# Squares for the DeltaNet norms as float16 high and low halves, summed by float16 products

## The reference

```
def l2norm(x):
    x32 = x.astype(jnp.float32)
    return x32 * lax.rsqrt(jnp.sum(x32 * x32, axis=-1, keepdims=True) + RMS_EPS)

def gated_deltanet_mixer(qkv, a_in, b_in, conv_w, a_log, dt_bias):
    qkv = jax.nn.silu(causal_depthwise_conv(qkv, conv_w))
    q, k, v = jnp.split(qkv, 3, axis=-1)
    q = l2norm(split_heads(q, B_HEADS, B_HEAD_DIM)) * (B_HEAD_DIM ** -0.5)
    k = l2norm(split_heads(k, B_HEADS, B_HEAD_DIM))
    ...
```

## Time and profile before

| | us |
|---|---|
| median of 3 runs | 652.02 |
| all runs | 651.27, 655.02, 652.02 |
| the profiled execution, its own time | 654.71 |
| its span (first to last instruction) | 652.6 |
| mean granted TensorE clock in it | 0.974 |
| PE busy | 589.1 (90% of the span) |
| DVE / ACT / POOL busy | 394.3 / 333.5 / 222.6 |

### The profile page before, as it was taken

The page is one execution under the profiler, slowest core; times in us unless marked ns, Lnnn a source line. Parts: engine busy times, 40 slices in busy tenths (PEclk is TensorE's granted clock), DMA queues, the critical chain, the costliest instruction groups (busy, mean ns, idle before and its releaser), DMA issues.

```text
span 652.6 us, 10019 instructions
## 1 busy us (share of the span) xinstructions
PE 589.1 (90%) x3763; PEld 368.8 (57%) x3763; DVE 394.3 (60%) x889; ACT 333.5 (51%) x585; POOL 222.6 (34%) x161
## 2 busy tenths in 40 slices
PE   3969988999999996999999999988988799799998
PEld 2424556756548653677677777754554466333443
DVE  6401487451687965786876557447799765577311
ACT  4625654425688768350812525346766677243510
POOL 0133453333044466042531530422221464242520
PEclk9998999989999899799999999979999999999999
DMA  8254764443113232120211110111120211162411
GB/s 321 63 127 111 155 123 130 138 153 113 51 50 113 66 98 65 33 65 2 65 33 32 53 46 1 46 53 51 36 78 34 66 33 43 56 228 74 145 55 48
DMA packets 31168, 53.04 MB, mean 81 GB/s; under 512 B 2743, under 2 KB 13201, under 8 KB 31121
## 3 DMA queue, kind: packets, MB, share of 16 engines
q1 hardware_dynamic: 30961, 52.27, 27.7%
q10 hardware_dynamic: 160, 0.14, 0.1%
HBM read 49.98 MB, written 2.42 MB: 80 GB/s over the span
## 4 chain that ended last, share of the span: by engine, by line
PE 67%; DVE 14%; ACT 8%; issue 5%; POOL 2%; DMA 2%; SPq 2%; DVEq 0%; ACTq 0%; PEldq 0%; POOLq 0%
PE bank L1790 12%; PE bank L1603 10%; PE bank L1605 9%; PE bank L1604 9%; PE bank L1858 5%; PE bank L1860 5%; PE bank L1862 5%; ACT stage L735 3%; PE bank L1639 2%; DMA stage<-in_w_in 2%; PE bank L1682 2%; POOL w_lo L518 1%; PE bank L1988 1%; PE bank L1821 1%; PE bank L1761 1%
## 5 line engine op out<-in xcount | busy, mean ns | idle before, releaser
L518 POOL TENSOR_TENSOR w_lo<-stage,w_hi 128x1024 f16<-128x1024 f32 (+4 forms) x76 | 149.1, 1964 | 250.9 <-ACT w_hi L743 250.9
L1790 PE MATMUL bank<-work 128*128 128x128 f32 x616 | 80.1, 280 | 8.1 <-DVEq L1298 7.8
L1790 PEld LDWEIGHTS bank<-work 128*128 128x128 f32 x616 | 77.7, 195 | 17.1 <-DVEq L1298 9.9
L743 ACT ACTIVATE w_hi<-stage 128x1024 f16<-128x1024 f32 (+4 forms) x76 | 74.5, 981 | 18.8 <-issue 14.4
L735 ACT ACTIVATE stage<-stage,small 128x512 f32<-128x512 f32 (+4 forms) x120 | 73.6, 662 | 8.1 <-DMA stage<-in_w_in 8.0
L1858 PE MATMUL bank<-hT_hi,w_hi 128*128 128x512 f16 x192 | 74.5, 388 | 1.7 <-PE bank L1862 0.9
L1860 PE MATMUL bank<-hT_lo,w_hi 128*128 128x512 f16 x192 | 74.2, 387 | 0.5 <-PE bank L1605 0.2
L1862 PE MATMUL bank<-hT_hi,w_lo 128*128 128x512 f16 x192 | 74.1, 386 | 0.3 <-PE bank L1605 0.2
L1603 PE MATMUL bank<-w_hi,hT_hi 128*128 128x260 f16 (+4 forms) x192 | 62.7, 327 | 9.1 <-POOL w_lo L518 6.4
L1604 PE MATMUL bank<-w_lo,hT_hi 128*128 128x260 f16 (+4 forms) x192 | 62.5, 326 | 0.0
L1605 PE MATMUL bank<-w_hi,hT_lo 128*128 128x260 f16 (+4 forms) x192 | 62.5, 325 | 0.0
(11 more groups left out here) (319 smaller groups left out, 1183.6 us busy)
## 6 DMA issues: line engine op xcount, KB each, us to landing
stage<-in_w_in SPq DMA_DIRECT2D x40, 512.0 KB, 3.5
stage<-in_c_phi_w SPq DMA_DIRECT2D x8, 512.0 KB, 4.0
stage<-in_w_branch SPq DMA_DIRECT2D x8, 512.0 KB, 3.7
stage<-in_w_out SPq DMA_DIRECT2D x8, 512.0 KB, 3.8
stage<-in_w_in SPq DMA_DIRECT2D x8, 260.0 KB, 2.8
strips<-rel_rows SPq DMA_DIRECT2D x8, 256.0 KB, 7.3
late<-in_x SPq DMA_DIRECT2D x1, 2048.0 KB, 10.1
out_x<-late SPq DMA_DIRECT2D x8, 256.0 KB, 2.0
```

The costliest lines, as they stand in the source:

```text
L518: gp.tensor_tensor(piece_view(w_lo[:, k % PAIRS, :], c), piece_view(stage[:, piece_at[c, j] % STAGES, :], c), piece_view(w_hi[:, k % PAIRS ...
L743: nc.scalar.activation(piece_view(w_hi[:, k % PAIRS, :], c), full, ACT.Copy).then_inc(hi_ready, 1)
L1790: ins = mm(ps[:, h * P:(h + 1) * P], lhs(h), rhs(h), start=True, stop=True)
```

## The change

For m = 0 to 7 the float32 square is now represented by two float16 numbers. ScalarE makes the high half, with one more ACTIVATE (`Square`, float16 output) right behind each `silu_conv(m)`; since it reads what that instruction wrote, it waits for it. GpSimd still makes the full square, now into `square_full`, waits for itself and for ScalarE's half, and subtracts the high half to get the low one. TensorE adds up both halves, eight float16 products with `ones_half` per m in the place of four float32 products. Sums 0 to 2 now stand after tile 1 of B3 and sum 3 after tile 3 of B3, in front of the "kcT" transpose; nothing stands between the tiles of B4. GpSimd's `squares_b(3)` moves up, between the second and third quarter of B4. Sums 4 to 7 stay inside tile 1 of B2.

```
         squares = early[:, 0:2048]
+        square_full = [early[:, 512 * n:512 * n + 512] for n in range(2)]
+        square_parts = early[:, 1024:3072].bitcast(f16).rearrange("p (s a n) -> p s a n", s=4, a=2)
...
             def squares_b(m):
                 gp.wait_ge(conv_done, m + 1)
-                if m >= 4:
-                    gp.wait_ge(sums_taken, m - 3)
-                gp.tensor_tensor(squares[:, 512 * (m % 4):512 * (m % 4) + 512], qkvT[:, m, 3:T + 3], qkvT[:, m, 3:T + 3],
-                                 ALU.mult).then_inc(SQ.sem, 1)
+                hold(gp.tensor_tensor(square_full[m % 2], qkvT[:, m, 3:T + 3], qkvT[:, m, 3:T + 3], ALU.mult))
+                gp.wait_ge(sq_hi_ready, m + 1)
+                gp.tensor_tensor(square_parts[:, m % 4, 1, :], square_full[m % 2], square_parts[:, m % 4, 0, :],
+                                 ALU.subtract).then_inc(SQ.sem, 1)
...
             for t in range(4):
                 follow(CH_B3, t)
-            squares_b(3)
+                if t == 1:
+                    squares_b(3)
...
                 nc.scalar.activation(qkvT[:, m, 3:T + 3], conv_bank[m % 2][:, :], ACT.Silu).then_inc(conv_done, 1)
+                if m < 8:
+                    act.wait_ge(conv_done, m + 1)
+                    if m >= 4:
+                        act.wait_ge(sums_taken, m - 3)
+                    nc.scalar.activation(square_parts[:, m % 4, 0, :], qkvT[:, m, 3:T + 3], ACT.Square).then_inc(sq_hi_ready, 1)
...
-            project(CH_B3, "B3", True)
+            def square_sums(ms):
+                ps = V.bank("sums")
+                for m in ms:
+                    SQ.wait(pe, ("B", m))
+                    for t in range(NT):
+                        c0 = 32 + 16 * (m // 4) + 4 * t + m % 4
+                        for a in range(2):
+                            ins = mm(ps[:, c0:c0 + 1], square_parts[:, m % 4, a, t * P:(t + 1) * P], ones_half[:, 0:1],
+                                     start=a == 0, stop=a == 1)
+                    ins.then_inc(sums_taken, 1)
+
+            def between_b3(t):
+                if t == 1:
+                    v_bank("sums")
+                    square_sums(range(3))
+                if t == 3:
+                    square_sums([3])
+
+            project(CH_B3, "B3", True, between=between_b3)
```

More of the change, by code:

```diff
@@ L166, in trunk @@
         ones = sb("ones", [P, P])
+        ones_half = sb("ones_half", [P, 2], f16)
         par = sb("par", [P, N_ROWS])
@@ L310, in trunk @@
         z_ready, sums_taken, gsum_ready = sem("z_gates_ready"), sem("squares_summed"), sem("log_decay_ready")
+        sq_hi_ready = sem("squares_hi_ready")
         gtri_ready = sem("cumulative_input_ready")
@@ L510, in hold @@
                 gp.wait_ge(p_step, step[0])
+            gp.memset(ones_half[:, :], 1.0)
             gp.memset(ones[:, :], 1.0).then_inc(fills, 1)
@@ L1812, in key_products @@
                 four(("qk", c), kc_, qc)
[L1815 to L1828, removed]
             def between_b2(t):
@@ L1843, in within_b2 @@
                     square_sums([4 + k // 2])
-            project(CH_B4, "B4", True, between=between_b4)
+            project(CH_B4, "B4", True)
             project(CH_B2, "B2", False, between=between_b2, within=within_b2)
```

## The result

The change makes the kernel slower. The changed kernel takes 659.04 us (median of 4 runs, 658.41 to 659.84), the kernel before 652.38 beside it (4 runs, 651.27 to 655.02): ratio 1.0091, 95% interval 1.0071 to 1.0111. The prediction was 657.4 (652.6 to 660.5), with 0.64 for slower by more than 0.5%. The profiled execution took 658.41, its span is 656.6.

A forecast was written before the change was run, and what follows sets the result against it. The prediction took the chain through ScalarE and GpSimd to L1273 and L1304, not TensorE, as the bound. 1.1 + 2.3 + 2.0 = +5.4 us gave 657.4 from the 652.02 median (660.1 from the profiled execution), range 652.6 to 660.5.

The forecast's parts named there:

- ScalarE: Squares behind silu in B1, B3 and B4: +1.14, +0.57 and +1.14, in all +2.85 us at B4's tile 0; m = 6 +0.7.
- The gap: ScalarE's 3.10 us idle before B4's tile 1 closes as TensorE is early, leaving 2.85 - 3.10 = -0.25 us.
- GpSimd's pairs: Square plus subtraction, 2.15 us per m (2.05 to 2.25); in B2 TensorE waits for them, +1.1 us at L1273.
- TensorE's sums: Eight float16 products take 0.25 us per m; TensorE gains about 4.4 us in B4 and 2.2 in B2.
- Keys' norm: VectorE's small compressed-keys instructions wait for GpSimd, making conv(4) and silu 4 late: +2.3 us (0 to 3).
- Norm factors: VectorE's small instructions behind L1273 wait for GpSimd's work up to its lo_split: +2.0 us (0 to 2.8).
- Rival 4: Clock falls to 1.2 GHz in B2's tile 1 while TensorE waits: +1.8 us, so 659.2; chance 0.12.
- Rival 3: Faster: ScalarE's gap closes, nothing replaces it; 649.4 us, decided at 1.45 us per GpSimd pair in B2; chance 0.08.
- the signs that the prediction named: No 3 us idle before B4's tile 1, about 2 before silu 4, slow VectorE instructions, waits at sums 4 to 7, B4 at full clock.

The follow-up runs named there:

- x5: Changed kernel with squares_b(3) back behind B4's fourth quarter and its sum after B4's tile 0; 657.44 us, ratio 1.0061 to the kernel before.
- x7: Changed kernel with GpSimd's first lo_split of G0 made to wait for the first decay matrix; 656.45 us, ratio 1.0058 to the kernel before.
- x9: Changed kernel with square 3 back behind B4's quarters, its sum after B4's tile 0, and G0's first lo_split behind the norm-factor chain; 656.01 us, ratio 1.0042.
- x6: Kernel before, its places kept, with GpSimd's one square written as float16 and one float16 product on TensorE, no low halves; 650.93 us, ratio 0.9963.
- x4: Changed kernel without low halves: GpSimd neither squares nor subtracts for m = 0 to 7, TensorE makes one product; 651.61 us, ratio 0.9975.

## Why the prediction came out right, step by step

The direction, the place and the mechanism were right. The total hides two errors of opposite sign, a stall taken 1.2 us too long and a gap taken 1.6 us too long, so that it came within 0.5 us (5.4 predicted, 5.9 by the ratio) is in part luck.

- **ScalarE.** Each Square takes 0.63 us as the earlier trace rows said. In B1 the two cost 0.92 on the ruler, not 1.14. At the drain of B4's tile 0 ScalarE is 3.67 us late, of which 1.06 are the keys' stall, so 2.61 for the Squares where 2.85 stood. Up to the last `lo_split` of B2 m = 6 adds 0.65, for 0.7.
- **The gap.** It closed in full, as predicted. But "3.10" was a property of one execution. In the second profile of before it is 1.48. The step that failed is "the gap closes and 2.85 - 3.10 = -0.25 is left": right against the profiled execution, and 1.6 us too favourable against the median. Carrying the sum over to the median by subtracting 2.69 us from the total took no account of where these 2.69 lie, and 1.6 of them lay in the stage of the change.
- **GpSimd's pairs.** Predicted 2.15 (2.05 to 2.25), measured 2.24 (232.15 to 238.87 for three); the four took 9.04 us (232.15 to 241.19), for 8.6. From the drain of B4's tile 1 to the copy of the sums the time grew by 23.82 - 22.16 = 1.66 us; predicted 1.35. The waits of 0.56 to 1.12 at the sums are as described.
- **TensorE's sums.** Eight float16 products take 0.35 us from first to last, for 0.25 predicted, and 24 take 0.75, so 0.03 each. The Trainium skill's 107 ns per load (TensorE: Matmul & The Clock Gate, LDWEIGHTS) would make 24 of them 2.6 us, as an estimate; the row decides, as it did in the prediction. It changes nothing in the sum, since TensorE waits.
- **Keys' norm.** Predicted 2.3, measured 1.06 as ScalarE's wait and 1.24 by taking it away. This is the mis-sized term. L1018 and L1235 were held to the ends of GpSimd's square (205.76) and subtraction (206.99), L1238's first instruction to that of the `lo_split` behind them (208.12); but two others passed in between, L1020 (TENSOR_SCALAR, 31 x 1) even while the subtraction ran. The seven were through at 208.3, where quarter 3's split was just starting, and not at 210.0.
- **Norm factors.** Predicted 2.0, measured 6.95 - 4.78 = 2.17, and 1.96 by taking it away.

Against the profile on which it was built the sum is +5.4 predicted and +4.33 measured: +2.05 and +0.50 at the drain of B4's tile 1, +1.35 and +1.66 up to the copy of the sums, +2.0 and +2.17 in the chain. Against the second profile of before the +5.91 are accounted for by runs to within 0.1: 1.24 keys' norm (x5), 1.88 norm factors (x7; 1.96 against the second profile of the changed kernel), and 2.71 that remain in x9: 0.83 at the drain of B4's tile 1 for the Squares net of the gap, 1.66 for GpSimd's pairs in B2, and 0.22 in the chain, where L1286 still takes 0.42 instead of 0.18. The Squares' share and the pairs' are read from places in the trace; no run took away one of them alone.

Behind the first decay matrix nothing is gained or lost: from there to the end of the span it is 407.0 and 407.3 us in the two profiles of the changed kernel and 407.0 and 406.7 in those of before. Rival 4, the clock falling in B2's tile 1, did not occur: the windows from 220 to 240 are at 1.00, even though TensorE is busy only 6.01 and 6.89 us in them. In x5 and x7 the clock did fall in the window from 220 to 230 (0.83), and neither stage was longer for it: x7 stands at the copy of the sums where the changed kernel does, within 0.1 us. Rival 3's turning point, 1.45 us a pair, was not measured; one float16 square of about 1.0 us per m (x6) and nothing at all (x4) both lie on its faster side, and both kernels are faster than before.

Of the signs that the prediction named, these came: no idle time before B4's tile 1, the wait before silu 4 (1.06 us for about 2), TensorE's waits at sums 4 to 7, and small VectorE instructions of 0.5 to 2 us, though only some of them. One did not: B4 did not run at full clock. The window from 210 to 220 is at 0.87, and with the one before it that makes 3.4 us at 1.2 GHz. It cost nothing here, since ScalarE came to the drain of tile 1 without idle time all the same.

## What to carry to other kernels

Shorter work on an engine pays only up to the next engine in line: here some 4 us less work on TensorE (584.2 us busy; 588.1 in the second profile of before, 589.1 in the first) became waiting, since the engine that had to prepare its operands, GpSimd, was already full for 9.5 of 10 us. A long instruction on GpSimd has a second price, paid by small VectorE instructions beside it: look for chains of 0.2 us instructions on the path and keep GpSimd quiet while they run, with work that isn't due yet behind them and not ahead. And where the profiled execution lies away from the median, find out with a second profile in which stage the difference sits before a gap in that stage is spent.

## What the hardware showed unexpectedly

- The same 32 float32 products, behind the same work to within 0.04 us, took 5.52 and 3.63 us in two executions of the same kernel, with 6.8 and 3.4 us at 1.2 GHz in the window. What decides between the two was not found.
- Small VectorE instructions differ in what they wait for. Beside a GpSimd subtraction a TENSOR_SCALAR of 31 x 1 took 0.14 us and a TENSOR_TENSOR of 31 x 1 behind it 0.84; a COPY of 128 x 16 took 2.11 beside a `lo_split` and 0.17 without.
- Beside VectorE's additions of the indexer's scores GpSimd's square takes 1.49 us instead of 1.04 and its subtraction 1.48 instead of 1.15 (from 193.78 on), while three of those additions take 4.22, so 1.41 each, where one alone takes 0.75. The square of before shows the same at that place (1.49, with three additions in 4.10), so only the subtraction can be a cost of the change there.
